# First rows of attention: moving one unit's fp16 split and one row of square sums behind the first attention rows

## The reference

```
q = (rms_norm(c_q) @ w_uq)  -> 16 heads x 96      k = (rms_norm(c_kv) @ w_ukv, shared rotary key) -> 16 x 96
q, k = rms_norm over each head, rotary on the last 32
s = q k^T * scale, causal;  p = softmax(s);  o = p v;  out = x + (o * silu(z)) @ w_out
```

## Time and profile before

| | |
|---|---|
| time, median of 3 runs | 961.25 us (960.92 to 961.68) |
| the profiled execution, its own time | 961.61 us |
| its span, first to last instruction | 959.8 us |
| PE busy | 946.7 us, 99% |
| DVE busy | 813.1 us, 85% |
| ACT busy | 574.2 us, 60% |
| POOL busy | 353.4 us, 37% |
| granted TensorE clock | 1.000 |

### The profile page before, as it was taken

The page is one execution under the profiler, slowest core; times in us unless marked ns, Lnnn a source line. Parts: engine busy times, 40 slices in busy tenths (PEclk is TensorE's granted clock), DMA queues, the critical chain, the costliest instruction groups (busy, mean ns, idle before and its releaser), DMA issues.

```text
span 959.8 us, 17260 instructions
## 1 busy us (share of the span) xinstructions
PE 946.7 (99%) x6406; PEld 670.4 (70%) x6406; DVE 813.1 (85%) x1412; ACT 574.2 (60%) x1074; POOL 353.4 (37%) x393
## 2 busy tenths in 40 slices
PE   9999999999999999999999999999999999999998
PEld 8788544444688888644457999997788888887443
DVE  5798899899865579988887899999999999998763
ACT  7343544424433454454646888876899988997230
POOL 0002234222000002234412577876652478894220
PEclk9999999999999999999999999999999999999999
DMA  9220422111054422332123264566565766460231
GB/s 306 42 64 23 110 73 60 44 44 43 3 175 149 158 67 67 98 122 50 39 72 111 79 204 151 212 183 177 117 169 144 169 151 117 84 181 2 88 110 66
DMA packets 165347, 103.74 MB, mean 108 GB/s; under 512 B 75272, under 2 KB 149520, under 8 KB 165008
## 3 DMA queue, kind: packets, MB, share of 16 engines
q1 hardware_dynamic: 159216, 102.25, 37.9%
q10 hardware_dynamic: 6048, 0.39, 0.5%
HBM read 56.48 MB, written 29.36 MB: 89 GB/s over the span
## 4 chain that ended last, share of the span: by engine, by line
PE 72%; DVE 20%; POOL 3%; issue 3%; ACT 2%; DVEq 0%; POOLq 0%; ACTq 0%
PE banks L111 20%; PE banks L113 19%; PE banks L112 19%; PE banks L2751 6%; PE banks L2769 2%; PE banks L2771 2%; PE banks L2770 2%; DVE heads_y L2498 1%; POOL heads_prod L2639 1%; DVE heads_x L2493 1%; DVE front_lt L1223 1%; DVE heads_x L2494 1%; DVE heads_ss L2543 1%; ACT front_set_b L723 1%; PE banks L2779 1%
## 5 line engine op out<-in xcount | busy, mean ns | idle before, releaser
L2515 DVE TENSOR_TENSOR heads_pt_lo<-banks,heads_pt_hi 128x512 f16<-128x512 f32 (+2 forms) x192 | 102.0, 553 | 10.3 <-ACT heads_pt_hi L2360 7.2
L2360 ACT ACTIVATE heads_pt_hi<-banks 128x512 f16<-128x512 f32 (+2 forms) x192 | 88.8, 486 | 8.5 <-PE banks L2751 8.3
L2507 DVE CUSTOM_DVE_ANT_0 heads_probs_big<-banks,heads_mask,score_scale 128x1024 f32<-128x1024 f32 (+1 forms) x64 | 68.6, 1071 | 2.9 <-PE banks L113 2.7
L2771 PE MATMUL banks<-heads_v,heads_pt_lo 128*128 128x64 f16 x576 | 70.5, 193 | 0.0
L2751 PE MATMUL banks<-ident,heads_probs_big 128*128 128x128 f32 x416 | 68.7, 278 | 1.8 <-DVE heads_pt_lo L2515 1.0
L2770 PE MATMUL banks<-heads_v,heads_pt_hi 128*128 128x64 f16 x576 | 70.5, 193 | 0.0
L2769 PE MATMUL banks<-heads_v,heads_pt_hi 128*128 128x64 f16 x576 | 70.4, 193 | 0.0
L2351 ACT ACTIVATE heads_probs_big<-heads_probs_big,heads_neg_max 128x1024 f32<-128x1024 f32 (+1 forms) x64 | 63.3, 989 | 8.5 <-DVE heads_neg_max L2507 7.5
L111 PE MATMUL banks<-heads_k_t,heads_q_t 96*128 96x512 f16 (+2 forms) x192 | 62.9, 328 | 1.7 <-DVE heads_neg_max L2507 1.7
L111 PE MATMUL banks<-front_act_hi,front_w_hi 128*128 128x512 f32 x160 | 63.8, 399 | 0.0
L113 PE MATMUL banks<-front_act_hi,front_w_lo 128*128 128x512 f32 x160 | 62.4, 390 | 0.0
(11 more groups left out here) (491 smaller groups left out, 3113.8 us busy)
## 6 DMA issues: line engine op xcount, KB each, us to landing
qk_scratch<-heads_y SPq DMA_DIRECT2D x22, 512.0 KB, 3.8
front_x<-in_x_t SPq DMA_DIRECT2D x16, 512.0 KB, 5.4
front_raw<-in_w_in_ab SPq DMA_DIRECT2D x14, 512.0 KB, 5.1
qk_scratch<-heads_last_y SPq DMA_DIRECT2D x10, 512.0 KB, 4.2
front_w<-in_w_out_ab SPq DMA_DIRECT2D x8, 512.0 KB, 3.8
x_scratch<-front_x SPq DMA_DIRECT2D x8, 512.0 KB, 3.9
v_scratch<-heads_v SPq DMA_DIRECT2D x32, 128.0 KB, 3.0
heads_v_st<-v_scratch SPq DMA_DIRECT2D x8, 512.0 KB, 5.2
```

Source lines behind the costliest of these rows:

```text
L2360: nc.scalar.activation(pt_hi[:, q % PIECES, :width], t_ps[:, banks[("piece", n, k)] % 3, :width], ACT.Copy).then_inc(pt_high, 1)
L2507: nc.vector.tensor_tensor_reduce(probs(n, 0, width), scores(i, 0, width), mask[:, S - width:], score_scale[:], 3e38, ALU.add, ALU.min, neg ...
L2515: nc.vector.tensor_tensor(pt_lo[:, q % PIECES, :width], t_ps[:, banks[("piece", n, k)] % 3, :width], pt_hi[:, q % PIECES, :width], ALU.sub ...
L2771: last = nc.tensor.matmul(o_part, pt_lo[:, q % PIECES, blk], v2[e][:, j, :VH], start=False, stop=(j == i))
```

## The change

In ACT's list, the high part of unit 25's split goes from the end of step 31 to behind the exponentials of row 2, in step 0 of attention. In DVE's list, the low part of unit 25's split goes from the end of step 31 to behind the low parts of row 1, in step 1 of attention, and q's sums of unit 31 go from behind the maxima of row 2 to behind the low parts of row 0. SP's, POOL's and PE's lists stay as they are. No instruction is added or dropped.

```diff
@@ scalar
             if u == UNITS - 2:
                 for n in range(AHEAD):
                     exponentials(n)
-            if u == UNITS - 1:
-                head_split(split_in(UNITS - 2))
@@ for n in range(N + BEHIND): high(n, k) ...
             if n + AHEAD < N:
                 exponentials(n + AHEAD)
+            if n == 0:
+                head_split(split_in(UNITS - 2))
@@ vector
+        def query_sums(u):
+            dve.wait_ge(q_squared, u + 1 + (u == UNITS - 1))
+            nc.vector.tensor_reduce(ss[:, u % QUAD, 0], q_squares(u), AX_X, ALU.add).then_inc(reduced, 1)
@@ for u in range(UNITS)
             if u == UNITS - 1:
                 maxima(AHEAD)
-            dve.wait_ge(q_squared, u + 1 + last_unit)
-            nc.vector.tensor_reduce(ss[:, j, 0], q_squares(u), AX_X, ALU.add).then_inc(reduced, 1)
+            if not last_unit:
+                query_sums(u)
...
-            if last_unit:
-                head_split(split_in(UNITS - 2))
@@ for n in range(N + BEHIND + TURN_LAG + 1): maxima(n + AHEAD) ...
                 for k in range(len(pieces(tile_of(n)[1]))):
                     low(n, k)
+                if n == 0:
+                    query_sums(UNITS - 1)
+                if n == 1:
+                    head_split(split_in(UNITS - 2))
```

## The result

The changed kernel takes 965.47 us (median of 6, 964.86 to 967.54) against 961.2 (median of 6); the ratio is 1.0045, interval 1.0032 to 1.0058. It is 4.3 us slower. The forecast was 962.3 within 961.0 to 964.2, so the direction was right and the size was not. The execution that was profiled is the longest of the six, 967.54. Its score tile 2 begins at 660.73, 0.74 later than in before, and over all the profiles of kernels that leave PE's start alone that moment lies between 658.88 and 660.73.

A forecast was written before the change was run, and what follows sets the result against it. DVE was taken as the bound from row 2's maxima to row 8's, then PE. Late q makes tile 10 1.57 us late, less 0.48 of slack about 1.1; 961.25 + 1.1 gives 962.3 us, range 961.0 to 964.2.

The forecast's parts named there:

- The bound and the reordering: First attention rows: DVE bounds up to row 8's maxima; reordered ACT and DVE lists make row 4's maxima 0.31 us late.
- PE's visible 0.7 us gain: Transposes of row 2 on PE begin at 665.45 instead of 666.16; costed at nothing, as PE then waits at tile 6.
- The issue order: SP's queue: the late store of unit 25 delays q of head 1 behind it to 669.50, 2.65 us later.
- The landing: q of head 1 takes 5.1 us to land, at about 674.6, so score tile 8 begins at 674.7.
- the step from tile 8 to the end: Lateness behind score tile 8 reaches the end as 1.1 us, by PE's path and by DVE's alike.
- the slack of 0.48 in PE's list: PE, tiles 12 to 13: 2.96 us against 2.48 for the same shapes later; absorbs 0.48 of 1.57 us lateness.
- DVE as the second path: Row 8's maxima on DVE begin 1.1 us later, at 676.2, and delay PE through ACT's exponentials of row 10.
- The spread that the prediction took its bounds from: Transfer times in before's trace: q 4.5 to 6.6 us, longest k 7.7, giving losses of 0.5, 2.6 and 3.7 us.
- Rival D: Behind score tile 8: PE's clock halves after its stop, 3.34 us take 6.7, total 965.7 us; chance 0.04.
- the forecast's stop: PE stands idle some 2.5 us ahead of score tile 8, three times its longest pause there.
- 0.5 us of slack: Before the change, q of head 1 landed at 671.95, 0.52 us ahead of score tile 8 at 672.47.

The follow-up runs named there:

- run 1: The changed kernel with the transfer of q of head 1 ahead of the store of unit 25 in SP's list; 961.35 us, ratio 1.0002.
- run 4: The kernel before with q of head 1 held in SP's list for the low part of row 1; 960.86 us, ratio 0.9997.
- run 5: The kernel before with q of head 1 held in SP's list for the first low part of row 2; 965.14 us, ratio 1.0038.
- Run 10: The changed kernel with 16 fp16 matmuls of 512 columns on PE in its wait for q of head 1; 963.63 us, ratio 1.0026.
- run 7: The changed kernel with 80 small extra matmuls of 8 columns at PE's very start; 996.02 us, ratio 1.0368.
- run 9: The changed kernel with 32 float32 transposes of 128 columns on PE in its wait for q of head 1; 964.91 us, ratio 1.0037.
- run 8: The kernel before with 80 small extra matmuls of 8 columns at PE's very start; 994.82 us, ratio 1.0349.

## Why the prediction was right and wrong

*The bound and the reordering: right.* The transposes of row 2 begin at 665.46 by before's scale (forecast 665.45), the low part of row 1 waits 0.23 (0.3), the maxima of row 4 are 0.28 late (0.31), and run 1 shows 0.29 us as their whole price. That PE's visible 0.7 us gain is worth nothing is shown by run 1 too.

*The issue order: right.* The store goes at 668.22 and q of head 1 at 669.47 by that scale (forecast 668.25 and 669.50). Runs 1, 4 and 5 show that q's lateness is necessary and enough.

*The landing: the term that was mis-sized.* The prediction said "I take 5.1, since the same three transfers go in the same order and distance". It took 6.4; over the runs, 4.2 to 6.5. This is the first step that failed. Put into the prediction's own working, 6.4 makes tile 8 begin at 676.0 and the loss 2.4 us. Run 10, which has this landing and no fallen clock, lost 2.6 in its profile and 2.2 by its median. So the step from tile 8 to the end, with the slack of 0.48 in PE's list and DVE as the second path, held. What the working lacked is that the same transfer can meet other traffic when it goes 2.6 us later: in before it lay clear of a fetch by luck. The spread that the prediction took its bounds from is largely this: in before's trace the landings over 5.1 us are those with a fetch in them, and that could have been read beforehand.

*The clock: a rival at 0.04 that happened.* This is the step that failed most: the forecast's sum has nothing for the clock behind tile 8. Of the 4.3 us, 1.1 were forecast, the long landing adds 1.3 and the clock some 2; with the landing alone the time would have been some 963.6, as in run 10. Rival D put 3.3 us on the halved clock behind tile 8, on top of the forecast's stop. The clock fell in the profile, where tiles 8 to 10 took 6.44 us (D had 6.7), and by the mean granted clock in at least four of the six runs of the changed kernel: those have 0.996, which none of 60 executions of before has. The other two have 0.998, as 11 of those 60 do, so that alone doesn't place a fall behind tile 8. Run 10 puts some 2 us on it by the medians, 2.6 in the profiles. The price came out lower than D's because a part of it was paid in slack, and in two of the six runs the mean clock lost only half as much. D's sum, 965.7, lies next to the measured 965.47 by some luck: its clock is over by more than 1 us and its stop under by about as much. The reason for 0.04 was that no row showed a low clock in attention; but no row showed PE stopped for 2 us there either, so the trace was silent and not against it. The Trainium skill, "TensorE: Matmul & The Clock Gate", section "What's actually happening", had it: an idle PE has its clock halved. The trace agrees, with 0.50 from 676.5 to 683.3 behind a stop of 3.53 us, and by this rule D deserved more than 0.04 once the forecast had PE stop.

*The two errors are linked, but not one.* With a 5.1 us landing the stop would have been some 2.3 us (an estimate: the queue's 669.47 + 5.1 against PE's last work, which ended at 672.4 by that scale), and no run shows what the clock does behind such a stop. In run 7, with a landing of 4.9 but a later issue, it was 2.94 and the clock fell even so, but for less: 0.50 from 707.9 to 711.3, 3.4 us and not 6.8. The long landing lengthened the stop, and the clock fell behind the stop.

What stays open: by how much a stop must be shorter for the clock to hold, what sets the time of a fetch, and run 9's time outside the span.

## What to carry to other kernels

Ahead of moving work on a busy engine, list what waits for its result on the queues that issue transfers, and what stands behind that wait; here moving a 0.9 us split, which saved nothing, moved a transfer by 2.6 us that had 0.5 us of slack. A wait that is named after one engine can have a second one right under it, so look up when each transfer landed. When a forecast has the tensor engine stop for some microseconds, count the clock behind the stop as part of the same case, and take a landing as the spread of its kind and not as its last value. Look, too, at what sets that spread: here it could be split by whether a fetch of instructions began in the transfer. And compare medians with medians: the one profile of before had a DVE split near its shortest, and other executions of the same lists had it 0.6 us longer.

## What the runs showed of the hardware

A fetch of instructions and a transposing transfer can meet: with one 16 KB fetch in their midst, 19 to 23 packets of 256 bytes took 1.3 to 1.8 us each, and the transfer 5.9 to 6.5 us and not 4.2 to 5.1.

DVE's low part of a split and POOL's instructions do not overlap freely: with a POOL instruction running, the split ended 0.81 us behind that instruction's end (157 cases), and took up to 1.58 us for 0.95. It holds the other way round too: in before, POOL's cast that began 0.1 us behind DVE's split took 1.34 us, and 0.61 where no split ran.

PE can be busy by its rows and have a low clock. In run 8, the control, these are the 80 extra matmuls of 8 columns at PE's start (the trace has two for each), and the clock of a stretch within them:

```profile
8.01 29.04 PE L1644 MATMUL banks<-front_ones 128*128 128x8 f32 x160
```

```profile
20.00:30.00 10.00, 10.00 (x48) 10.00 (x48) 9.17 (x9) 9.74 (x10) 0.00 (x0) 0.50 0.69 142
```

PE was busy for all of these 10 us by its rows, and the granted clock was 0.50. The 80 matmuls, 29 us long, made attention begin 30.4 us later.
